# First block's attention by pairs of heads: two heads share TensorE's row halves and column halves, in steps of two units

## The chip, the core and the metric

One Trainium2 core runs the whole program in one launch. Its engines run on their own and meet through semaphores: TensorE (PE; PEld is its weight load), VectorE (DVE), ScalarE (ACT), GpSimd (POOL) and SyncE (SP), which issues the transfers. The metric is the device time of one execution in microseconds, the median of several.

## What is computed

Two transformer blocks, each two layers deep, on one sequence of 256 tokens of width 1024. The change touches the first block's attention alone. Cut to that:

```python
def attention(q, k, v, scale):          # 256 queries in blocks of 128
    def one_block(qi):
        s = jnp.einsum('bhgqd,bhkd->bhgqk', qi, k) * scale
        p = jax.nn.softmax(s, axis=-1)
        return jnp.einsum('bhgqk,bhkd->bhgqd', p, v)

for i in range(2):                       # first_block
    ...                                  # projections, norms, rope
    og = attention(qg, kg, vg, ...)      # GQA: 6 heads of 64, 2 key heads, 3 query heads to a key head
    om = attention(qm, km, vm, ...)      # MLA: 6 heads, 96 wide in q and k, 64 in v
    mix = concatenate([og, om, pooled]) @ w_out
```

In layer 0 attention is done twice: for the 256 context tokens (keys: the 256 context tokens) and for the 256 latent tokens (keys: all 512). In layer 1 only the latent tokens have queries. All of it is in float32.

## The kernel before

Every engine has its program written out in order; banks of PSUM (eight, 512 float32 wide) are handed out by `plan_banks` ahead of time, and an engine waits on a bank's semaphores `filled` and `drained`. Weights come through a ring of three 2 MB slots (`ring`), and SyncE issues the transfer into a slot when the last product of the slot's old weights has been issued.

Attention goes by **units**: one head, one set (context, or latent) and 128 queries. A set has 256 keys (two tiles of 128, context) or 512 (four tiles, latent). Layer 0 has 48 units (12 heads x 2 sets x 2 halves of the queries), layer 1 has 24. One unit passes through these stages, which the text names by letters:

- **S** (TensorE, L1229): scores, one product of 128 queries with 256 or 512 keys. A GQA head is 64 rows deep and lies in partitions 0 to 63 or 64 to 127 of `qT` and `kT` (`base = 64 * (h // 3)`); an MLA head is 96 rows deep.
- **R** (VectorE, L2024): the negative row maximum out of PSUM.
- **E** (ScalarE, L1599): exp with that maximum as bias, into `pb`, with the row sums; frees the score bank.
- **N** (VectorE, L2034, L2035): reciprocal of the sum, and scaling of the weights in `pb`.
- **T** (TensorE, L1241): the weights transposed, tile by tile.
- **C** (ScalarE, L1608): the transposed weights copied to `pT`.
- **V** (TensorE, L1255), once for two units (both halves of a head's queries): values, one product of 64 columns by 256 queries for each tile, accumulated.
- **O** (VectorE, L2044), once for two units: V's result copied to `mixT` (the same memory as `hT`).

The three loops run in steps of one unit. TensorE does S of unit u, T of unit u-2 and, every second step, V; VectorE R of u, N of u-1, O; ScalarE E of u, C of u-2. Scores have banks 0 to 2, transposes 3 and 4, values 5 and 6, by turns. In layer 0 TensorE also does eight rows of the modulation product in between (`mod_products`, L1066), each as two halves of four 512-column products, which write four strips of 32 columns; VectorE copies each row out (L1848). Bank 7 is theirs. A TensorE product in float32 shows as two matmul records (a transpose as one).

After attention follow, in layer 0, the transposed modulation rows (L1078), and in both layers the pooled part (L1268), the output projection (L1124) and the MLP.

Of the kernel before, what the change touches and what calls it, by code (L numbers as in the profile page):

```python
# [11 lines left out]
ALU = mybir.AluOpType  # L12
ACT = mybir.ActivationFunctionType
# [43 lines left out]
ATTN_STEPS = 6  # L57
# [120 lines left out]

def plan_banks():
# [24 lines left out]
    for i in range(DEPTH):  # L204
# [14 lines left out]
        u = 0  # L219
        pair = 0  # L220
        for h in range(GQ + MH):
            for s in range(len(sets_of(i))):
                for qt in range(2):
                    take((tag, "s", u), u % 3)
                    take((tag, "t", u), 3 + u % 2)
                    u += 1
                take((tag, "o", pair), 5 + pair % 2)
                pair += 1
# [154 lines left out]
def program(nc, A, out):  # L383
# [10 lines left out]
    with ExitStack() as ctx:  # L394
# [202 lines left out]
        def await_bank(eng, key):  # L597
            b, n = use[key]
            eng.wait_ge(filled[b], n + 1)

# [377 lines left out]
        def _(pe):  # L978
# [151 lines left out]
            for i in range(DEPTH):  # L1130
# [76 lines left out]
                sets = sets_of(i)  # L1207
                units = [(h, s, qt) for h in range(GQ + MH) for s in range(len(sets)) for qt in range(2)]
# [4 lines left out]
                ru[0] += len(units)  # L1213
                for s_ in range(len(units) + 4):
                    if s_ < len(units):
                        h, s, qt = units[s_]
                        if h == GQ and s == 0 and qt == 0:
# [4 lines left out]
                        q0, tiles = sets[s][0] + qt * P, sets[s][1]  # L1222
                        b = start_bank((tag, "s", s_))
                        if h < GQ:
                            base = 64 * (h // 3)
                            lhs, rhs = qT[base:base + HD, h % 3, q0:q0 + P], kT[base:base + HD, 0:tiles * P]
                        else:
                            lhs, rhs = qmT[0:MQK, h - GQ, q0:q0 + P], kmT[0:MQK, h - GQ, 0:tiles * P]
                        fill(mm(b[:, 0:tiles * P], lhs, rhs, start=True, stop=True), (tag, "s", s_))  # L1229


                    n, step = divmod(s_, ATTN_STEPS)
                    if i == 0 and n < MOD_ATTN and step in (2, 4):
                        mod_products(MOD_FIRST + n, range(0, 4) if step == 2 else range(4, KC))
                    u = s_ - 2
                    if 0 <= u < len(units):
                        h, s, qt = units[u]
                        b = start_bank((tag, "t", u))
                        pe.wait_ge(p_ready, p_base + u + 1)
                        for j in range(sets[s][1]):  # L1240
                            last = tr(b[:, j * P:(j + 1) * P], pb[:, u % 3, j * P:(j + 1) * P], IDENT)  # L1241
                        fill(last, (tag, "t", u))
                    u = s_ - 3
                    if 0 <= u < len(units) and u % 2 == 1:
                        h, s, _ = units[u]
                        pair = u // 2
                        b = start_bank((tag, "o", pair))
                        await_drained(pe, (tag, "t", u - 1))
                        await_drained(pe, (tag, "t", u))
                        base = 64 * (h % 2)  # L1250
                        tiles = sets[s][1]
                        for j in range(tiles):
                            v = v_tok[:, j, HD * (h // 3):HD * (h // 3) + HD] if h < GQ else \
                                vm_tok[:, j, MV * (h - GQ):MV * (h - GQ) + MV]
                            last = mm(b[base:base + 64, 0:SEQ], v, pT[:, pair % 2, j, :],  # L1255
                                      start=(j == 0), stop=(j == tiles - 1))
                        fill(last, (tag, "o", pair))
# [14 lines left out]
                npair = len(units) // 2  # L1272
                await_drained(pe, (tag, "o", npair - 1))
                await_drained(pe, (tag, "o", npair - 2))
# [173 lines left out]
        def _(act):  # L1448
# [116 lines left out]
            for i in range(DEPTH):  # L1565
# [20 lines left out]
                sets = sets_of(i)  # L1586
                units = [(h, s, qt) for h in range(GQ + MH) for s in range(len(sets)) for qt in range(2)]
                base = sum(24 * len(sets_of(j)) for j in range(i))
                for s_ in range(len(units) + 2):
                    if s_ < len(units):  # L1590
                        u = s_
                        h, s, qt = units[u]
                        keys = sets[s][1] * P
                        act.wait_ge(nmax_ready, base + u + 1)
                        if u >= 3:

                            await_bank(act, (tag, "t", u - 3))
                        st = stat[:, 8 * (u % 4):8 * (u % 4) + 8]
                        drain(act_fn(pb[:, u % 3, 0:keys], bank((tag, "s", u))[:, 0:keys], ACT.Exp, bias=st[:, 2:3],  # L1599
                                     accum_out=st[:, 4:5]), (tag, "s", u))  # L1600
                    u = s_ - 2
                    if 0 <= u:
                        h, s, qt = units[u]
                        tiles, pair = sets[s][1], u // 2
                        await_bank(act, (tag, "t", u))
                        if pair >= 2:
                            await_bank(act, (tag, "o", pair - 2))
                        drain(act_fn(pT[:, pair % 2, 0:tiles, qt * P:(qt + 1) * P],  # L1608
                                     bank((tag, "t", u))[:, 0:tiles * P].rearrange("p (j q) -> p j q", j=tiles),
                                     ACT.Copy), (tag, "t", u))  # L1610
# [162 lines left out]
        def _(dve):  # L1773
# [227 lines left out]
            for i in range(DEPTH):  # L2001
# [13 lines left out]
                sets = sets_of(i)  # L2015
                units = [(h, s, qt) for h in range(GQ + MH) for s in range(len(sets)) for qt in range(2)]
                for s_ in range(len(units) + 4):
                    if s_ < len(units):
                        u = s_
                        h, s, qt = units[u]  # L2020
                        keys = sets[s][1] * P
                        st = stat[:, 8 * (u % 4):8 * (u % 4) + 8]
                        await_bank(dve, (tag, "s", u))
                        V.tensor_reduce(st[:, 2:3], bank((tag, "s", u))[:, 0:keys], AX_X, ALU.max, negate=True)\  # L2024
                            .then_inc(nmax_ready, 1)
                    if i == 0 and s_ and s_ % ATTN_STEPS == 0 and s_ // ATTN_STEPS <= MOD_ATTN:
                        mod_row_copied(MOD_FIRST + s_ // ATTN_STEPS - 1)
# [232 lines left out]
```

## Time and profile before

| | |
|---|---|
| median of 3 runs | 2026.58 us (2022.17 to 2028.48) |
| profiled execution | 2027.55 us, its span 2025.7 us |
| busy in the span | PE 1897.6 us (94%), PEld 1499.4, DVE 1104.3, ACT 885.2, POOL 398.1 |
| attention of layer 0 | 193.2 to 306.9 us of the span |
| attention of layer 1 | 885.3 to 955.7 us of the span |

A matmul's record lasts until its last result is written, so records of one engine overlap: what an instruction costs TensorE is the distance to the next start. Granted clock 1.00 is 2.4 GHz, 0.50 is 1.2 GHz. A row's bracket says how long the engine was idle before it, and who released it.

### The profile page before, as it was taken

The page shows a single profiled execution, that of the slowest core. Times are in us where ns is not written, and L with a number is a line of the kernel's source. Part 1 is how long each engine was busy: PE and PEld are TensorE (multiplying, and loading weights), DVE is VectorE, ACT ScalarE, POOL GpSimd, SP SyncE. Part 2 cuts the span into 40 slices and gives each one's busy share as a digit, 9 for nine tenths or more (in the row PEclk, how much of TensorE's full clock was granted, in tenths as well). Part 3 has the DMA queues.
Part 4 walks back from the last instruction along what each step waited for, and adds up shares of the span by engine and source line. Part 5 has one row for each costly group of instructions (what it writes and reads, how often), then busy time and mean ns, then how long its engine had stood idle before and what let it go on. Part 6 is the DMA issues. An engine that isn't in the chain of part 4 may idle for free.

```text
span 2025.7 us, 28617 instructions
## 1 busy us (share of the span) xinstructions
PE 1897.6 (94%) x10840; PEld 1499.4 (74%) x10840; DVE 1104.3 (55%) x1948; ACT 885.2 (44%) x1757; POOL 398.1 (20%) x834
## 2 busy tenths in 40 slices
PE   4999999899999998999999989988999799989998
PEld 2443445388888885634899989877899798878898
DVE  3317551377777633354355557566555575665554
ACT  2226440242423333353355556455554364555542
POOL 1014100000000000140000006035453142254523
PEclk8899997899999999989899999999999899999999
DMA  8311440235455431300344532532244334323351
GB/s 297 127 51 42 158 165 2 83 136 197 168 191 182 166 83 32 117 1 1 116 176 172 197 131 95 207 126 84 97 154 169 123 137 166 126 84 126 126 171 59
DMA packets 139875, 255.26 MB, mean 126 GB/s; under 512 B 14926, under 2 KB 21724, under 8 KB 139612
## 3 DMA queue, kind: packets, MB, share of 16 engines
q1 hardware_dynamic: 138742, 251.16, 35.7%
q8 instruction: 88, 1.44, 0.3%
q0 software_dynamic: 704, 2.10, 0.3%
q14 instruction: 47, 0.39, 0.1%
q10 hardware_dynamic: 294, 0.18, 0.0%
HBM read 252.38 MB, written 1.05 MB: 125 GB/s over the span
## 4 chain that ended last, share of the span: by engine, by line
PE 82%; DVE 7%; ACT 4%; issue 3%; POOL 1%; SPq 1%; DMA 1%; ACTq 0%; DVEq 0%; POOLq 0%
PE ps L1115 16%; PE ps L1117 15%; PE ps L1116 15%; PE ps L1124 10%; PE ps L1009 3%; PE ps L1229 3%; PE ps L1255 3%; PE ps L1241 2%; PE ps L1026 1%; PE ps L1324 1%; PE ps L1326 1%; PE ps L1325 1%; PE ps L1089 1%; PE ps L1066 1%; SPq L790 1%
## 5 line engine op out<-in xcount | busy, mean ns | idle before, releaser
L1915 DVE TENSOR_TENSOR big_r<-ring,big_r 128x1024 fp32r<-128x1024 f32 x198 | 245.1, 1239 | 257.9 <-ACT big_r L1505 257.4
L1505 ACT ACTIVATE big_r<-ring 128x1024 fp32r<-128x1024 f32 x198 | 209.4, 1059 | 386.9 <-PE ps L1117 378.2
L1116 PE MATMUL ps<-big_r 128*128 128x256 f32 (+1 forms) x1120 | 374.0, 334 | 0.0
L1115 PE MATMUL ps<-hT_r,big_r 128*128 128x256 f32 (+1 forms) x896 | 290.8, 325 | 11.2 <-DVE big_r L1924 10.9
L1117 PE MATMUL ps<-hT_r,big_r 128*128 128x256 f32 (+1 forms) x896 | 283.4, 316 | 0.0
L1116 PEld LDWEIGHTS ps<-big_r 128*128 128x128 f32 x1120 | 215.2, 192 | 19.1
L1124 PE MATMUL ps<-hT,ring 128*128 128x512 f32 (+2 forms) x576 | 207.4, 520 | 10.7 <-ACT hT L1526 8.9
L1115 PE MATMUL ps<-big_r 128*128 128x256 f32 (+1 forms) x592 | 195.6, 330 | 1.4 <-DVE big_r L2070 1.4
L1117 PE MATMUL ps<-big_r 128*128 128x256 f32 (+1 forms) x592 | 194.6, 329 | 0.0
L1115 PEld LDWEIGHTS ps<-hT_r,big_r 128*128 128x128 f32 x896 | 173.1, 193 | 27.7 <-issue 11.8
L1124 PEld LDWEIGHTS ps<-hT,ring 128*128 128x128 f32 (+1 forms) x576 | 109.3, 192 | 105.7 <-issue 95.0
L1117 PEld LDWEIGHTS ps<-hT_r,big_r 128*128 128x128 f32 x896 | 173.2, 193 | 10.4
L1915 DVE TENSOR_TENSOR cst_r<-ring,w_ukv_sb_r 128x1024 fp32r<-128x1024 f32 x70 | 87.5, 1250 | 116.2 <-ACT w_ukv_sb_r L1505 116.2
L1115 PEld LDWEIGHTS ps<-big_r 128*128 128x128 f32 x592 | 112.5, 190 | 12.0 <-DVE big_r L2070 2.2
L1117 PEld LDWEIGHTS ps<-big_r 128*128 128x128 f32 x592 | 112.5, 190 | 10.0
L1881 DVE SCALAR_TENSOR_TENSOR pT<-ring,csilu,pT 128x512 f32<-128x512 f32 x168 | 118.5, 747 | 1.3
L1115 PE MATMUL ps<-hT_r,w_ukv_sb_r 128*128 128x256 f32 x384 | 114.6, 299 | 0.0
L894 POOL MEMSET big<- 128x1088 f32 x2 | 2.0, 1014 | 560.3 <-PE ps L1117 560.3
L1505 ACT ACTIVATE w_ukv_sb_r<-ring 128x1024 fp32r<-128x1024 f32 x70 | 74.1, 1058 | 85.4 <-PE ps L1117 72.6
L1117 PE MATMUL ps<-hT_r,cst_r 128*128 128x256 f32 x384 | 110.1, 287 | 0.0
L1116 PE MATMUL ps<-xT_r,w_ukv_sb_r 128*128 128x256 f32 x384 | 110.0, 286 | 0.0
L1898 DVE SCALAR_TENSOR_TENSOR nt<-ps,nt 128x256 f32<-128x256 f32 (+3 forms) x74 | 39.0, 527 | 125.3 <-ACT nt L1477 125.0
(278 smaller groups left out, 4205.7 us busy)
## 6 DMA issues: line engine op xcount, KB each, us to landing
ring<-in_w_in SPq DMA_DIRECT2D x42, 2048.0 KB, 7.8
ring<-in_w_mlp SPq DMA_DIRECT2D x32, 2048.0 KB, 7.8
ring<-in_w_mod SPq DMA_DIRECT2D x24, 2048.0 KB, 8.0
ring<-in_w_out SPq DMA_DIRECT2D x4, 2048.0 KB, 8.1
ring<-in_w_out_a SPq DMA_DIRECT2D x4, 2048.0 KB, 7.8
ring<-in_w_out_b SPq DMA_DIRECT2D x4, 2048.0 KB, 7.9
ring<-in_w_o SPq DMA_DIRECT2D x4, 2048.0 KB, 8.4
ring<-in_w_in SPq DMA_DIRECT2D x12, 256.0 KB, 5.0
```

Of the source, the lines that this page charges most:

```text
L1009: last = mm(b[0:parts, 0:T], ones, sq[0:parts, n % SQ, 0:T], start=(j == 0), stop=(j == chunks - 1))
L1115: mm(b[:, 0:T], w_hi[:, k, :], hi(k), start=(k == 0), stop=False)
L1116: mm(b[:, 0:T], w_hi[:, k, :], lo(k), start=False, stop=False)
L1117: last = mm(b[:, 0:T], w_lo[:, k, :], hi(k), start=False, stop=(k == KC - 1))
L1124: last = mm(b[0:cols, 0:T], w[:, k, m:m + cols], src(k), start=(k == 0), stop=(k == KC - 1))
L1229: fill(mm(b[:, 0:tiles * P], lhs, rhs, start=True, stop=True), (tag, "s", s_))
L1241: last = tr(b[:, j * P:(j + 1) * P], pb[:, u % 3, j * P:(j + 1) * P], IDENT)
L1255: last = mm(b[base:base + 64, 0:SEQ], v, pT[:, pair % 2, j, :], start=(j == 0), stop=(j == tiles - 1))
L1505: act_fn(hi, raw, ACT.Copy).then_inc(hi_ready, 1)
L1881: ins = V.scalar_tensor_tensor(acc, w, c, acc, ALU.mult, ALU.add)
L1898: drain(V.scalar_tensor_tensor(r2, bank(key)[0:parts, 0:T], width * EPS, r2, ALU.add, ALU.mult), key)
L1915: V.tensor_tensor(lo, raw, hi.bitcast(F32), ALU.subtract).then_inc(lo_ready, 1)
```

## The change

Attention now goes by **groups** (two heads, one set) in **steps** (one half of the group's queries, so two units, one of each head). The GQA pairs are heads h and h+3, whose rows are the two halves of the partitions and which belong to different key heads; the MLA pairs are neighbours. A step's two S are issued back to back into two banks. V takes both heads of a group, tile by tile in turn, into the two halves of one bank's partitions (an even head 0 to 63, an odd one 64 to 127). Scores have banks 0 to 3, transposes 4 and 5, values bank 6 alone. The fourth buffer for weights is a part of `sq`; the transposed weights of odd groups go to `rstd` and `nt`, which ScalarE may overwrite once the last MLA key unit is drained, for which it now waits at the start. O of a GQA group is two copies of 64 partitions, of an MLA group one of 128. ScalarE does C of step j-2 ahead of E of step j; before, E came first. The modulation halves come at the second and third of every three steps.

```diff
-ATTN_STEPS = 6
+ATTN_STEPS = 3
...
+HEAD_PAIRS = [(h, h + GQ // 2) for h in range(GQ // 2)] + [(GQ + h, GQ + h + 1) for h in range(0, MH, 2)]
+def groups_of(i):
+    return [(pair, s) for pair in HEAD_PAIRS for s in range(len(sets_of(i)))]
...
+        for u in range(4 * len(groups_of(i))):
+            take((tag, "s", u), u % 4)
+            take((tag, "t", u), 4 + u % 2)
+        for g in range(len(groups_of(i))):
+            take((tag, "o", g), 6)
...
+        def weights(u):
+            return pb[:, u % 4, :] if u % 4 < 3 else sq[:, 2, :]
+        def weights_T(g, e):
+            return pT[:, e, :, :] if g % 2 == 0 else (rstd, nt)[e][:, :, :].rearrange("p a (b c) -> p (a b) c", b=2)
...
+                for j in range(steps + 3):
+                    if j < steps:
+                        pair, s = groups[j // 2]
...
+                        q0, tiles = sets[s][0] + j % 2 * P, sets[s][1]
+                        banks = [start_bank((tag, "s", 2 * j + e)) for e in range(2)]
+                        for e, h in enumerate(pair):
+                            if h < GQ:
+                                rows = slice(HD * (h // 3), HD * (h // 3) + HD)
+                                lhs, rhs = qT[rows, h % 3, q0:q0 + P], kT[rows, 0:tiles * P]
...
+                            fill(mm(banks[e][:, 0:tiles * P], lhs, rhs, start=True, stop=True), (tag, "s", 2 * j + e))
...
+                    n, step = divmod(j, ATTN_STEPS)
+                    if i == 0 and n < MOD_ATTN and step:
+                        mod_products(MOD_FIRST + n, range(0, 4) if step == 1 else range(4, KC))
+                    if 0 <= j - 2 < steps:
+                        tiles = sets[groups[(j - 2) // 2][1]][1]
+                        for u in (2 * j - 4, 2 * j - 3):
+                            b = start_bank((tag, "t", u))
+                            pe.wait_ge(p_ready, p_base + u + 1)
...
+                    g, odd = divmod(j - 4, 2)
+                    if 0 <= g < len(groups) and not odd:
...
+                        for t in range(tiles):
+                            for e, h in enumerate(pair):
+                                rows = slice(64 * (h % 2), 64 * (h % 2) + 64)
...
+                                last = mm(b[rows, 0:SEQ], v, weights_T(g, e)[:, t, :], start=(t == 0), stop=(t == tiles - 1))
...
+                await_drained(act, (tag, f"km{MH - 1}", 0))
+                for j in range(steps + 2):
+                    if j >= 2:
...
+                        for e in range(2):
+                            key = (tag, "t", 2 * j - 4 + e)
+                            await_bank(act, key)
...
+                    if j < steps:
...
+                            act.wait_ge(nmax_ready, base + u + 1)
...
+                for j in range(steps + 3):
+                    if j < steps:
+                        keys = sets[groups[j // 2][1]][1] * P
+                        for u in (2 * j, 2 * j + 1):
...
+                            await_bank(dve, (tag, "s", u))
...
+                    if 1 <= j <= steps:
...
+                        for u in (2 * j - 2, 2 * j - 1):
...
+                            await_drained(dve, (tag, "s", u))
...
+                    g, odd = divmod(j - 4, 2)
+                    if 0 <= g < len(groups) and not odd:
...
+                        await_bank(dve, key)
+                        if pair[0] < GQ:
+                            for h in pair:
+                                rows = slice(64 * (h % 2), 64 * (h % 2) + 64)
+                                last = V.tensor_copy(mixT[rows, h // 2, q0:q0 + SEQ], bank(key)[rows, 0:SEQ])
+                        else:
+                            last = V.tensor_copy(mixT[:, pair[0] // 2, q0:q0 + SEQ], bank(key)[:, 0:SEQ])
```

TensorE's order in the GQA heads of layer 1, before (a pair of units; `x4` are four transposes or the four tiles of V):

```order
L1229 MATMUL ps<-big 128x512
L1241 MATMUL ps<-cst,pb 128x128 x4
L1229 MATMUL ps<-big 128x512
L1241 MATMUL ps<-cst,pb 128x128 x4
L1255 MATMUL ps<-pT,big 64x256 x4
```

and of the change, one group, at the same place (S is L1243, T is L1255, V is L1269; this group's transposed weights are those of `pT`):

```order
L1243 MATMUL ps<-big 128x512 x2
L1255 MATMUL ps<-cst,pb 128x128 x4
L1255 MATMUL ps<-cst,sq 128x128 x4
L1243 MATMUL ps<-big 128x512 x2
L1255 MATMUL ps<-cst,pb 128x128 x8
L1269 MATMUL ps<-pT,big 64x256 x8
```

Two S stand together, two units' transposes stand together, and V's eight products of a group stand where four of a head stood.

VectorE's order at the same place, before (two heads):

```order
L2024 TENSOR_REDUCE stat<-ps 128x1
L2034 RECIPROCAL stat<-stat 128x1
L2035 TENSOR_SCALAR pb<-pb,stat 128x512
L2044 COPY hT<-ps 64x256
L2024 TENSOR_REDUCE stat<-ps 128x1
L2034 RECIPROCAL stat<-stat 128x1
L2035 TENSOR_SCALAR pb<-pb,stat 128x512
```

and of the change (R is L2034, N is L2043 and L2044, O is L2055):

```order
L2034 TENSOR_REDUCE stat<-ps 128x1 x2
L2043 RECIPROCAL stat<-stat 128x1
L2044 TENSOR_SCALAR pb<-pb,stat 128x512
L2043 RECIPROCAL stat<-stat 128x1
L2044 TENSOR_SCALAR sq<-sq,stat 128x512
L2055 COPY hT<-ps 64x256 x2
L2034 TENSOR_REDUCE stat<-ps 128x1 x2
L2043 RECIPROCAL stat<-stat 128x1
L2044 TENSOR_SCALAR pb<-pb,stat 128x512
L2043 RECIPROCAL stat<-stat 128x1
L2044 TENSOR_SCALAR pb<-pb,stat 128x512
```

R of a step's two units now stands ahead of both N of the step before, and O's two copies follow every second N pair.

## Rows read from the trace of the kernel before

**Rows 1.** Windows: stretch, busy us by engine (instructions), granted clock, DMA share, GB/s.

```profile
193.20:307.00 113.80, 109.48 (x514) 50.27 (x514) 65.57 (x177) 51.04 (x145) 17.95 (x23) 1.00 0.42 148
...
885.30:898.00 12.70, 12.61 (x23) 4.97 (x22) 6.17 (x14) 4.28 (x11) 9.74 (x15) 0.50 0.00 0
898.00:955.70 57.70, 54.49 (x220) 27.42 (x219) 28.63 (x71) 26.29 (x62) 0.00 (x0) 0.98 0.00 1
```

**Rows 2.** TensorE's timeline, layer 1, GQA: start, us, engine, line, shapes, [idle].

```profile
906.12 1.12 PE L1229 MATMUL ps<-big 64*128 64x512 f32 x2
907.18 0.66 PE L1241 MATMUL ps<-cst,pb 128*128 128x128 f32 x4
907.76 1.12 PE L1229 MATMUL ps<-big 64*128 64x512 f32 x2
...
909.42 1.92 PE L1255 MATMUL ps<-pT,big 128*64 128x256 f32 x8
911.28 1.12 PE L1229 MATMUL ps<-big 64*128 64x512 f32 x2
```

**Rows 3.** The same, layer 1, MLA; the last row two pairs later.

```profile
921.56 1.12 PE L1229 MATMUL ps<-big 96*128 96x512 f32 x2
922.52 0.60 PE L1241 MATMUL ps<-cst,pb 128*128 128x128 f32 x4
922.96 1.02 PE L1229 MATMUL ps<-big 96*128 96x512 f32 x2
...
931.84 1.12 PE L1229 MATMUL ps<-big 96*128 96x512 f32 x2
```

**Rows 4.** TensorE's timeline, layer 0, GQA, around a half modulation row (L1066).

```profile
226.54 0.44 PE L1241 MATMUL ps<-cst,pb 128*128 128x128 f32 x2
226.90 0.70 PE L1229 MATMUL ps<-big 64*128 64x256 f32 x2
227.53 1.07 PE L1066 MATMUL ps<-ring,cwide 128*32 128x512 f32 x8
228.53 0.66 PE L1241 MATMUL ps<-cst,pb 128*128 128x128 f32 x4
229.11 1.08 PE L1255 MATMUL ps<-pT,big 128*64 128x256 f32 x4
230.12 0.70 PE L1229 MATMUL ps<-big 64*128 64x256 f32 x2
```

**Rows 5.** The same, layer 0: latent V of one head and of the ninth after.

```profile
213.95 1.94 PE L1255 MATMUL ps<-pT,big 128*64 128x256 f32 x8
...
297.56 1.94 PE L1255 MATMUL ps<-pT,big 128*64 128x256 f32 x8
```

**Rows 6.** TensorE's timeline, second block: two 64-row products, what comes next.

```profile
1314.06 0.37 PE L1399 MATMUL ps<-big 64*128 64x128 f32 x1
1314.07 0.37 PE L1400 MATMUL ps<-big 64*128 64x128 f32 x1
...
1314.48 0.23 PE L1401 MATMUL ps<-mask_bf,ident_bf 128*128 128x128 bf16 x1
```

**Rows 7.** VectorE's timeline, layer 1, MLA: R, reciprocal, scaling, O.

```profile
933.00 0.69 DVE L2024 TENSOR_REDUCE stat<-ps 128x1 f32<-128x512 f32 x1 [2.08 <-PE ps L1229]
933.61 0.15 DVE L2034 RECIPROCAL stat<-stat 128x1 f32<-128x1 f32 x1
933.80 0.49 DVE L2035 TENSOR_SCALAR pb<-pb,stat 128x512 f32<-128x512 f32 x1
934.20 0.41 DVE L2044 COPY hT<-ps 64x256 f32<-64x256 f32 x1
```

**Rows 8.** ScalarE's timeline at the same place: E, C.

```profile
933.73 0.69 ACT L1599 ACTIVATE pb<-ps,stat 128x512 f32<-128x512 f32 x1 [2.10 <-DVE stat L2024]
...
934.41 0.59 ACT L1608 ACTIVATE pT<-ps 128x512 f32<-128x512 f32 x1
```

More of the change, by code:

```diff
@@ L1204, in _ @@
                 run_units(tag, units_a(i) + units_m(i), main)
-                sets = sets_of(i)
-                units = [(h, s, qt) for h in range(GQ + MH) for s in range(len(sets)) for qt in range(2)]
+                sets, groups = sets_of(i), groups_of(i)
+                steps = 2 * len(groups)
                 pe.wait_ge(roped, roped_before(tag, 1))
@@ L1212, in _ @@
                 p_base = ru[0]
[L1213 to L1217, printed above, removed]
+                ru[0] += 2 * steps
+                for j in range(steps + 3):
+                    if j < steps:
+                        pair, s = groups[j // 2]
+                        if pair[0] == GQ and s == 0 and j % 2 == 0:
                             pe.wait_ge(roped, roped_before(tag, 1) + 2 * MH)
@@ L1229, in _ @@
[L1229 to L1250, printed above, removed]
-                        tiles = sets[s][1]
[L1252 to L1257, printed above, removed]
+                        q0, tiles = sets[s][0] + j % 2 * P, sets[s][1]
@@ new lines, in _ @@
+                    n, step = divmod(j, ATTN_STEPS)
[7 more added lines that the diff above has]
+                            for t in range(tiles):
+                                last = tr(b[:, t * P:(t + 1) * P], weights(u)[:, t * P:(t + 1) * P], IDENT)
+                            fill(last, (tag, "t", u))
@@ L1270, in _ @@
                     fill(last, key)
[L1272 to L1274 removed]
+                await_drained(pe, (tag, "o", len(groups) - 1))
                 await_drained(pe, (tag, "pool", 1))
@@ L1584, in _ @@
                 run_units(tag, units_a(i) + units_m(i))
-                sets = sets_of(i)
-                units = [(h, s, qt) for h in range(GQ + MH) for s in range(len(sets)) for qt in range(2)]
+                sets, groups = sets_of(i), groups_of(i)
+                steps = 2 * len(groups)
                 base = sum(24 * len(sets_of(j)) for j in range(i))
[L1589 to L1610, printed above, removed]
@@ L2014, in _ @@
                 run_units(tag, units_a(i) + units_m(i))
[L2015 to L2027, printed above, removed]
-                    u = s_ - 1
-                    if 0 <= u < len(units):
-                        h, s, qt = units[u]
-                        keys = sets[s][1] * P
-                        st = stat[:, 8 * (u % 4):8 * (u % 4) + 8]
-                        await_drained(dve, (tag, "s", u))
-                        link(V.reciprocal(st[:, 6:7], st[:, 4:5]))
-                        V.tensor_scalar(pb[:, u % 3, 0:keys], pb[:, u % 3, 0:keys], st[:, 6:7], None, ALU.mult)\
-                            .then_inc(p_ready, 1)
-                    u = s_ - 4
-                    if 0 <= u and u % 2 == 1:
-                        h, s, _ = units[u]
@@ L2046, in _ @@
+                        drain(last, key)
                 if i == 0:
```

58 lines of the change are left out of this document (37 added, 21 removed).

## Prediction

> **What bounds the kernel now.** I read the windows first, then TensorE's timeline in steady attention, then VectorE's and ScalarE's. The letters S, R, E, N, T, C, V, O are those of the section on the kernel. In layer 0's attention (113.8 us) TensorE is busy 109.48 us, VectorE 65.57 and ScalarE 51.04; in layer 1's (12.7 + 57.7 us) TensorE is busy 67.1 us, VectorE 34.8, ScalarE 30.6 [rows 1]. What has to be seen next is whether that busy time is work. It is: in a GQA pair of layer 1 every phase starts where the one before has issued its columns, S 1.06 us, T 0.58, S, T, then V 1.86, a pair of units in 5.16 us [rows 2]. MLA has the same period, (931.84 - 921.56) / 2 = 5.14 us, with S 0.96 and T 0.44 [rows 3]. Layer 0 shows the short pieces: T of two tiles 0.36, S of 256 columns 0.63, half a modulation row 1.00, V of two tiles 1.01 [rows 4], and a whole head, its share of the eight modulation rows included, takes (297.56 - 213.95) / 9 = 9.29 us [rows 5]. Twelve heads are 111.5 us of the 113.7 from 193.2 to 306.9; twelve pairs are 61.8 us of layer 1's 70.4. So attention is bound by what TensorE issues, the rest being ends and, in layer 1, a start at half clock. What shortens S and V shortens the kernel; what shortens VectorE or ScalarE does not.
>
> **The GQA scores.** Heads h and h+3 stand in the two row halves, and their two S are now issued back to back into two banks. The trace has that form elsewhere: the second block's two 64-row score products start 0.01 us apart, and the next instruction starts 0.42 us after the first [rows 6]; one after the other, two products of 128 columns would have taken that twice less one change of phase. I therefore take a GQA pair's S at the price of one: 1.06 us (latent set) or 0.63 (context set). The other bound is two in a row, which is rival A. MLA's S fills 96 rows and stays double: at most 2 x 0.96 = 1.92, and for 256 columns 0.10 less than the GQA form, 2 x 0.53 = 1.06.
>
> **The values.** Two heads go to column halves, interleaved tile by tile. No row shows two 64-column products side by side, but the half modulation row is four 512-column products into four strips of 32 columns in 1.00 us [rows 4], where one 512-column S alone takes 1.06 [rows 2]. So column strips share the time of one. Bounds: 1.86 for both heads (one price) and 3.72 (no sharing); I take 1.86, the strip row being nearly the same operation, and 1.01 for the context set.
>
> **The transposes.** Their number is unchanged, but two units now stand together. The second costs what tiles alone add: 0.58 - 0.36 = 0.22 for two tiles [rows 2, 4], 0.44 for four, against 0.36 and 0.58 apart. A step's T is 1.02 (latent) or 0.58 (context); in MLA I take 0.88 for one step and 1.02 for the one that goes before V.
>
> **The sum for TensorE.** A group is two heads of one set: two steps of S, two of T, one V.
> GQA, latent: 2 x 1.06 + 2 x 1.02 + 1.86 = 6.02 us (before: 10.32).
> GQA, context: 2 x 0.63 + 2 x 0.58 + 1.01 = 3.43.
> MLA, latent: 2 x 1.92 + 0.88 + 1.02 + 1.86 = 7.60 (before: 10.28).
> MLA, context: 2 x 1.06 + 2 x 0.58 + 1.01 = 4.29.
> Layer 0: 3 x (6.02 + 3.43) + 3 x (7.60 + 4.29) + 16 half rows x 1.00 = 80.0 us against 111.5: -31.5.
> Layer 1: 3 x 6.02 + 3 x 7.60 = 40.9 against 61.8: -20.9.
>
> **What the other queues then do.** VectorE's work hardly changes. From R to the reciprocal is 0.61 us, on to the scaling 0.19, on to the next 0.40, and a copy is 0.41 [rows 7]: a GQA latent group is 4 x 1.20 + 2 x 0.41 = 5.62 us, under 6.02. ScalarE's is 4 x (0.68 + 0.59) = 5.08 [rows 8]. In layer 0 their 65.57 and 51.04 us stand against 80. Both fit, but with little to spare in the three GQA groups of layer 1.
>
> What is queued behind each wait matters more. VectorE does R of step j+1 before N of step j, and every second step waits with O for V. Take a V that ends at time 0, with S of step j+1 behind it. R can begin 1.16 us after that S is issued (933.00 - 931.84 [rows 3, 7]); the two O copies, 0.82 us, lie inside these 1.16. R, R, reciprocal, scaling: 1.16 + 1.22 + 0.19 + 0.49 = 3.06 us until the first weights of step j are ready, 3.65 for the second. TensorE wants them after S, T, S: 1.06 + 1.02 + 1.06 = 3.14, and the second 0.44 later, at 3.58. So the transposes come within a tenth of a microsecond of waiting; with semaphore time I charge 0.3 us to each of the six GQA latent groups, 1.8 in all. In MLA TensorE arrives at 1.92 + 0.88 + 1.92 = 4.72 and waits for nothing; in layer 0 a half row lies in two steps of three and covers it, except beside a step without one. The other step parity has V in between. Four score banks let S of step j+2 wait only for E of step j, which ends more than a step earlier; the two transpose banks are drained by C within the next S and T. The single value bank is emptied two steps before its next use.
>
> ScalarE's new wait for the last MLA key unit costs nothing: VectorE drains that unit ahead of its first R in its own queue. The modulation slots are consumed every 10 us instead of 14, three deep, and the queue's 148 GB/s of that window [rows 1] becomes some 200. The last released slots belong to the output projection and are asked for several steps before the end.
>
> The start of layer 1 does change. Before, the clock is 0.50 (1.2 GHz) while only S and T run, and 0.98 on average from 898.0 on, where the first V begins [rows 1]. In the new order five steps' S and three steps' T lie ahead of the first V: 5 x 1.06 + 3 x 1.02 = 8.4 us, at half clock 16.7, against 12.7 before. If V is what raises the clock, that is about 4 us more at half rate, 2 us lost; if paired S raises it too, nothing. I take 1.0.
>
> Sum: -31.5 - 20.9 + 1.8 + 1.0 = -49.6. The profiled execution took 2027.55 us (span 2025.7), so 1978.0; the median of the runs is 1.0 lower, so **1977 us**.
>
> **Rivals.** *A, row halves take turns.* Then each GQA step pays S twice: 12 latent steps x 0.96 and 6 context steps x 0.53 give 14.7 us back: 1992. [Rows 6] speak against it. If the column halves took turns, 12 latent groups x 1.86 and 6 context groups x 1.01 give 28.4 back: 2005, and the strips in [rows 4] speak against that. Chance of either 0.05.
>
> *B, VectorE's queue sets the pace.* Margins of a tenth cannot be trusted: if each link of R, E, N and T is 0.2 us longer than in the rows, or VectorE runs slower beside GpSimd, TensorE waits about 0.8 us in each of the 18 groups: 14 us, 1991; spread 1987 to 2002. For it: 5.62 against 6.02. Against it: in MLA and in layer 0, where most of the gain is, TensorE still has 1 to 2 us of slack in a group. The Trainium skill, TensorEngine Tiling (Array Packing), section PSUM Bottleneck, warns of this very turn: packing speeds TensorE up and not the emptying of PSUM. [...] Chance 0.22.
>
> *C, slower: the clock falls inside attention.* The work is thinner in products and thicker in transposes: T takes 34% of a GQA group (2.04 of 6.02) where it took 22% (1.16 of 5.16). If TensorE then stayed at 1.2 GHz through both stages, the 80.0 and 40.9 us would double: 160 against 113.7 and 82 against 70.4, 58 us more than before: 2085. It decides from where some 50 of the 121 us run at half clock, since each costs another. For it: 885.3 to 898.0, when TensorE was busy 12.61 of 12.70 us with S and T at 0.50 [rows 1]. Against it: layer 0 holds 1.00 throughout with the same S, T and V, and each S and V now fills the whole array. The Trainium skill, TensorE: Matmul & The Clock Gate, Part 4 on transposes, says that a transpose does not count as busy for the clock as a product does; the trace's stretch before 898 fits that. Chance 0.04.
>
> *D, better than the sum.* The rows' prices contain a change of phase (S 1.06 against 0.96 in MLA), and a second S behind a first need not pay it. With 0.1 us less for each of some 60 phases, no stall and no late clock: 1969, at best 1964. Chance 0.08.
>
> **How the numbers follow.** The forecast's own case, 1967 to 1987, has 0.61. The range 1965 to 1992 adds most of D, A and half of B: about 0.8. Faster by over 0.3% (6 us, about what a measurement of this kernel can tell from no change) are all cases but C and a worse B: 0.94; within 0.3%: 0.02; slower: 0.04.
>
> **What would show it.** In the new trace the two GQA S must start together and be followed by T some 1.06 us later; V of two heads must take some 1.9 us for 16 matmul records of the latent set; a GQA latent group must last 6.0 to 6.4 us, an MLA one 7.4 to 7.7; layer 0's attention some 84 us, layer 1's some 50. Waits of T for the scaling above 0.5 us in every group would be B, a granted clock under 1.00 after layer 1's first 17 us C. I am wrong if time saved here returns later, which I see no wait for: the stages behind find their weights in the ring.

## The result, and the profile after

The changed kernel takes 1971.37 us (median of 4 runs, 1969.74 to 1972.63), the kernel before in the same session 2027.53 us (2022.17 to 2029.32): a ratio of 0.9727, 95% interval 0.9707 to 0.9747, 56.2 us less. Forecast were 1977 us and 49.6 us less, range 1965 to 1992. The profiled execution after has a span of 1967.9 us.

Where the time went, from the starts in the two timelines (attention counts from its first S to what follows it: the turned modulation rows in layer 0, the pooled part in layer 1), in us:

| stage | before | after | difference |
|---|---|---|---|
| run's start to the first block's first projection | 62.49 | 58.83 | -3.7 |
| from there to attention, layer 0 | 130.77 | 131.58 | +0.8 |
| attention, layer 0 | 113.60 | 83.51 | -30.1 |
| turned modulation rows | 11.64 | 12.05 | +0.4 |
| pooled part and output projection, layer 0 | 77.36 | 76.89 | -0.5 |
| MLP of layer 0, projections of layer 1 | 489.46 | 490.25 | +0.8 |
| attention, layer 1 | 70.33 | 45.72 | -24.6 |
| the rest | 1070.06 | 1069.08 | -1.0 |

The two attentions are 54.7 us less, and nothing comes back later. The first row lies ahead of anything that was edited, and its 3.7 us are chance: in the kernels further down, which begin with the same instructions, that stretch takes between 59.2 and 63.1 us.

The windows of the changed kernel, beside [rows 1] (columns as there; the first row is all of layer 0's attention, the second the turned modulation rows, the other three layer 1's attention):

```profile
190.40:273.90 83.50, 79.70 (x512) 39.28 (x512) 64.75 (x170) 48.07 (x144) 17.38 (x22) 1.00 0.57 202
273.90:285.60 11.70, 11.67 (x66) 11.55 (x64) 0.42 (x1) 0.00 (x0) 0.00 (x0) 0.60 0.01 4
853.10:857.60 4.50, 3.72 (x9) 1.21 (x9) 2.45 (x5) 1.47 (x5) 4.06 (x8) 0.61 0.00 0
857.60:865.50 7.90, 6.87 (x36) 3.42 (x36) 7.69 (x19) 6.69 (x17) 5.69 (x8) 1.00 0.00 1
865.50:898.80 33.30, 31.82 (x197) 19.02 (x196) 23.32 (x59) 21.10 (x52) 0.00 (x0) 1.00 0.00 1
```

The instruction counts are those of before (512 against 514 matmul records in layer 0), but TensorE is busy 79.70 us instead of 109.48: the same products, side by side. VectorE and ScalarE do nearly the same work (64.75 and 48.07 us, before 65.57 and 51.04) in 30 us less, and TensorE is still the engine that is busy nearly all the time. The third row holds the one term whose sign the forecast had wrong: at the start of layer 1 the clock is 0.61 on average for 4.5 us, where it was 0.50 for 12.7.

The profile models the ends of TensorE's records, so the prices below are distances from start to start. TensorE's timeline in the same place shows the new order (start, us, then the instruction; layer 1, the GQA groups and the first MLA step):

```profile
853.12 3.71 PE L1243 MATMUL ps<-big 64*128 64x512 f32 x8
857.61 1.13 PE L1243 MATMUL ps<-big 64*128 64x512 f32 x4 [0.79 <-ACT pb L1620]
859.26 1.40 PE L1255 MATMUL ps<-cst,pb 128*128 128x128 f32 x8 [0.52 <-DVE pb L2044]
860.59 1.13 PE L1243 MATMUL ps<-big 64*128 64x512 f32 x4
...
863.15 1.13 PE L1243 MATMUL ps<-big 64*128 64x512 f32 x4
864.39 1.22 PE L1255 MATMUL ps<-cst,pb 128*128 128x128 f32 x8
865.53 1.95 PE L1269 MATMUL ps<-pT,big 128*64 128x256 f32 x16
867.41 1.13 PE L1243 MATMUL ps<-big 64*128 64x512 f32 x4
868.47 0.65 PE L1255 MATMUL ps<-cst,pb 128*128 128x128 f32 x4
868.96 0.60 PE L1255 MATMUL ps<-cst,sq 128*128 128x128 f32 x4
869.40 1.88 PE L1243 MATMUL ps<-big 96*128 96x512 f32 x4
```

Four records of S, two heads, take 868.47 - 867.41 = 1.06 us, what two records took in [rows 2]. Sixteen records of V, two heads, take 867.41 - 865.53 = 1.88 us, what eight took. From S at 863.15 to S at 869.40 lie two S, two T of four tiles for each head, and one V, the work of a whole latent GQA group: 6.25 us, where 6.02 and, with waits, 6.0 to 6.4 were forecast. An MLA group further on:

```profile
873.97 1.98 PE L1243 MATMUL ps<-big 96*128 96x512 f32 x4
875.79 0.60 PE L1255 MATMUL ps<-cst,pb 128*128 128x128 f32 x4
876.23 0.60 PE L1255 MATMUL ps<-cst,sq 128*128 128x128 f32 x4
876.66 1.88 PE L1243 MATMUL ps<-big 96*128 96x512 f32 x4
878.38 1.04 PE L1255 MATMUL ps<-cst,pb 128*128 128x128 f32 x8
879.35 1.95 PE L1269 MATMUL ps<-pT,big 128*64 128x256 f32 x16
```

S 1.82 and 1.72, T 0.87 and 0.97, V 1.88 (to the next S at 881.23): 7.26 us, where two periods of [rows 3] took 10.28.

### The profile page after: what moved, and what is told of

It reads as the page before. It is cut to its first block, busy times and chain, and to the rows that moved or that the text cites. A ratio compares the mean times of both kernels' runs of the same rounds, so it can differ in the third digit from the quotient of the medians.

```text
span 1967.9 us, 28606 instructions
## 1 busy us (share of the span) xinstructions
PE 1840.9 (94%) x10840; PEld 1477.3 (75%) x10840; DVE 1101.7 (56%) x1939; ACT 881.7 (45%) x1757; POOL 397.6 (20%) x834
## 4 chain that ended last, share of the span: by engine, by line
PE 80%; DVE 8%; ACT 5%; issue 3%; POOL 1%; SPq 1%; DMA 1%; ACTq 0%; DVEq 0%; POOLq 0%
PE ps L1128 16%; PE ps L1130 15%; PE ps L1129 15%; PE ps L1137 10%; PE ps L1022 3%; PE ps L1243 2%; PE ps L1269 1%; PE ps L1039 1%; PE ps L1255 1%; PE ps L1335 1%; PE ps L1336 1%; PE ps L1337 1%; PE ps L1102 1%; SPq L803 1%; DVE big_r L1926 1%
## 5 line engine op out<-in xcount | busy, mean ns | idle before, releaser
L1128 PE MATMUL ps<-hT_r,big_r 128*128 128x256 f32 (+1 forms) x896 | 290.9, 325 | 10.9 <-DVE big_r L1935 10.6
L1137 PE MATMUL ps<-hT,ring 128*128 128x512 f32 (+2 forms) x576 | 207.2, 519 | 10.8 <-ACT hT L1537 9.2
```

The source lines that it names most:

```text
L1128: mm(b[:, 0:T], w_hi[:, k, :], hi(k), start=(k == 0), stop=False)
L1137: last = mm(b[0:cols, 0:T], w[:, k, m:m + cols], src(k), start=(k == 0), stop=(k == KC - 1))
```

## The experiments

"Attention stages" below are the two rows of the table, together 129.2 us in the changed kernel; medians are beside the changed kernel's 1971.37, ratios against the kernel before on the same chip.

### Which half is worth what

**One column half.** Both heads' values go into one half of the partitions, one head after the other:

```diff
-                        for t in range(tiles):
-                            for e, h in enumerate(pair):
-                                rows = slice(64 * (h % 2), 64 * (h % 2) + 64)
+                        for e, h in enumerate(pair):
+                            for t in range(tiles):
+                                cols = slice(SEQ * e, SEQ * e + SEQ)
...
-                                last = mm(b[rows, 0:SEQ], v, weights_T(g, e)[:, t, :], start=(t == 0), stop=(t == tiles - 1))
+                                last = mm(b[0:64, cols], v, weights_T(g, e)[:, t, :], start=(t == 0), stop=(t == tiles - 1))
...
```

> V of a group's two heads goes to the same column half (partitions 0 to 63, one head in columns 0 to 255 of the bank, the other behind it); everything else is as in the change. Theory (TensorE's columns are the bound and the halves share their time): V costs twice, 12 latent groups x 1.72 us and 6 context groups x 0.86, about +26 us against the change, near 1997. Rival (the order in steps of two and the fewer phases bring the gain, not the sharing): within 5 us of the change.

Measured: 1994.26 us (1993.69 to 1999.84), ratio 0.9859 [0.9815, 0.9903]; attention 99.74 and 56.01 us, 26.5 more. Its TensorE timeline, an MLA group of layer 1:

```profile
891.94 1.94 PE L1269 MATMUL ps<-rstd,big 128*64 128x256 f32 x8
893.71 1.89 PE L1269 MATMUL ps<-nt,big 128*64 128x256 f32 x8
895.53 1.98 PE L1243 MATMUL ps<-big 96*128 96x512 f32 x4
897.36 0.60 PE L1255 MATMUL ps<-cst,pb 128*128 128x128 f32 x4
897.79 0.60 PE L1255 MATMUL ps<-cst,sq 128*128 128x128 f32 x4
898.23 1.88 PE L1243 MATMUL ps<-big 96*128 96x512 f32 x4
899.95 1.04 PE L1255 MATMUL ps<-cst,pb 128*128 128x128 f32 x8
900.92 1.29 PE L1269 MATMUL ps<-pT,big 128*64 128x256 f32 x5
```

V now takes 3.59 us (891.94 to 895.53) against 1.88. Twelve latent groups of 1.71 are 20.5 us. A context V takes 1.87 us (221.23 to 223.10) against 1.01, and six of them are 5.2. Layer 0 also has 3.4 us at half clock (202.9 to 206.3) that the changed kernel does not have, at most 1.7 us. The column halves share fully, as [rows 4] said.

**Row pairs undone.** The GQA pairs are neighbours, so both heads lie in the same row half in two groups of three (the pair 2, 3 lies in both halves; it stands second here):

```diff
-HEAD_PAIRS = [(h, h + GQ // 2) for h in range(GQ // 2)] + [(GQ + h, GQ + h + 1) for h in range(0, MH, 2)]
+HEAD_PAIRS = [(0, 1), (2, 3), (4, 5)] + [(GQ + h, GQ + h + 1) for h in range(0, MH, 2)]
```

> GQA pairs are heads (0,1), (2,3), (4,5): only (2,3) spans both row halves, the other two pairs' S take turns. Theory: 8 latent steps x 0.85 and 4 context steps x 0.43 give 8.5 us back; and, because layer 1 now opens with S of one row half, its clock stays at 0.50 well beyond the 3 us that it takes in the change, some 4 to 6 us more: +13 in all, near 1984. Rival on the clock (it rises after a fixed time whatever S does): +8.5 and the clock up after about 3 us as in the change. Rival on S (row halves bring nothing): no change.

Measured: 1983.19 us (1979.84 to 1984.98), ratio 0.9803 [0.9766, 0.9841]; attention 94.95 and 51.52 us, 17.2 more.

**The same, with the shared pair first**, so that attention starts with S in both row halves:

```diff
-HEAD_PAIRS = [(h, h + GQ // 2) for h in range(GQ // 2)] + [(GQ + h, GQ + h + 1) for h in range(0, MH, 2)]
+HEAD_PAIRS = [(2, 3), (0, 1), (4, 5)] + [(GQ + h, GQ + h + 1) for h in range(0, MH, 2)]
```

> The same three pairs with (2,3) first, so that layer 1 opens with paired S. Both clock theories: +8.5 us against the change and the clock up about 3 us after attention's start in layer 1. The difference to the run with (0,1) first is what paired S at the start is worth to the clock: 4 to 6 us by the theory, 0 by the rival.

Measured: 1976.6 us (1974.67 to 1978.82), ratio 0.9773 [0.9735, 0.9811]; attention 88.19 and 47.49 us, 6.5 more. S of a pair that lies in one row half, from its timeline in layer 1:

```profile
866.62 1.98 PE L1243 MATMUL ps<-big 64*128 64x512 f32 x4
868.53 0.66 PE L1255 MATMUL ps<-cst,pb 128*128 128x128 f32 x4
```

That is 1.91 us where two S side by side take 1.06, the 0.85 a latent step that was expected. Eight latent and four context steps would be 8.5 us; where the missing 2 us went was not traced. Two of rival A's three pairs would be 9.8 us; 6.5 puts all three at some 10.

The two kernels do the same products in another order, and differ by 10.8 us. Windows of the first of them at the start of layer 1, where its first S starts at 863.53:

```profile
865.00:870.00 5.00, 5.00 (x8) 2.35 (x8) 2.07 (x3) 1.77 (x5) 4.56 (x8) 0.50 0.00 0
870.00:875.00 5.00, 4.84 (x15) 2.35 (x14) 4.13 (x10) 2.36 (x6) 3.48 (x5) 0.50 0.00 0
875.00:880.00 5.00, 5.00 (x17) 2.12 (x14) 3.68 (x11) 3.88 (x11) 0.00 (x0) 0.75 0.00 2
```

and of the second, where it starts at 859.15:

```profile
857.60:863.00 5.40, 5.21 (x12) 1.68 (x10) 1.86 (x4) 1.44 (x4) 4.96 (x9) 0.54 0.00 0
863.00:870.00 7.00, 6.36 (x25) 3.32 (x26) 6.82 (x16) 5.16 (x14) 6.24 (x9) 1.00 0.00 1
```

TensorE is busy without a gap in the first row of the first, and stays at 1.2 GHz; with two S side by side it is back at 2.4 GHz some 4 us after attention began. In layer 0, which the expectation left out, the first kernel also falls to half clock just behind its first S, for some 20 us (0.50 from 191.5 to 212.0, with TensorE busy throughout), and the second keeps 1.00. The clock is the difference that the two profiles show; whether the other order of the pairs costs anything besides is not shown. One more profile of each, unchanged:

> A second profile of the kernel that opens each layer with S of one row half. Theory (paired S raises the clock, S of one half does not): layer 1 again at 0.50 for 10 us or more after attention's start. Rival (the stretch at half clock is an accident of the moment): a stretch of another length, as short as 3 us.

> A second profile of the kernel that opens each layer with paired S. Theory: in layer 1 the clock is up within some 5 us of attention's start, and layer 0 stays at 1.00. Rival: any length up to 15 us.

Measured, one run each: 1983.8 and 1981.6 us; attention 94.95 and 49.87 us, against 89.09 and 47.49: 5.9 and 2.4 us apart, the same sign in both layers, smaller. In layer 1 the clock was low for some 10 and 7 us around the first S, and back 8.0 and 3.7 us behind it: the second is what the theory expected, the first falls short of its 10 us. In layer 0 the first kernel has its 20 us again; the second has 3.4 us at half clock (202.9 to 206.3), where the theory had 1.00 throughout. The medians of several runs above differ by 6.6 us.

All thirteen profiles of this case bear on the start of layer 1. Where it opens with two S side by side and the clock is low at the first S (eight profiles), the clock is back 1.8 to 4.2 us behind it; where it opens with S of one row half (the kernel before and both profiles of the first kernel here), 15.0, 14.0 and 8.0 us behind it. Two more open with paired S at full clock, and it falls later. Nor does S of one row half always bring the clock down: in layer 0 of the kernel before, where single S stand between modulation rows, T and V, it stays at 1.00.

**Both undone:**

> Both sharings mostly undone at once, the schedule kept: V of both heads in one column half, and GQA pairs (2,3), (0,1), (4,5), of which only the first spans both row halves. If the costs simply add: what the run with one column half gave back and what the run with (2,3) first gave back, +26 + 6 = some +32 us against the change, near 2002, which leaves some 20 to 25 us below the kernel before that neither sharing explains (joined phases, fewer waits, the start of layer 1). Rival (the halves are all of it): +50 us or more, at the kernel before within 0.5%.

Measured: 2003.87 us (2001.33 to 2005.38), ratio 0.988 [0.9845, 0.9916]; attention 103.58 and 57.78 us, 32.1 more than in the changed kernel. The parts nearly add up: 26.5 and 6.5. And this kernel, in which no two products of a pair of heads run together except in one GQA pair of three, is still 22.6 us under before in attention (161.4 against 183.9). One part of that is read from the MLA group above: 895.53 - 891.94 for V, 1.83 and 1.72 for S, 0.87 and 0.97 for T are 8.98 us, where [rows 3] have 10.28. S and T of two units stand together, and a phase that is twice as long is changed half as often: 1.3 us in each MLA latent group. The other part is layer 1's clock, low for 6.8 us around the first S instead of 17.0; within attention that is 3.7 us at half rate instead of 15.0, some 5.6 us less lost.

### Order and depth

**V head by head**, still in both column halves:

```diff
-                        for t in range(tiles):
-                            for e, h in enumerate(pair):
+                        for e, h in enumerate(pair):
+                            for t in range(tiles):
```

> V's two heads still go to the two column halves, but all tiles of the first head are issued before the second head's. Theory (products start in program order, so only the neighbours at the seam share): nearly as in the run with one column half, +20 to +26 us. Rival (TensorE runs the other half's products ahead): within 3 us of the change.

Measured: 1980.17 us (1977.28 to 1983.38), ratio 0.9791 [0.9753, 0.9829]; attention 89.01 and 51.17 us, 11.0 more. Neither theory gave that number. Its timeline, one V of layer 1 (`rstd` holds the first head's weights, `nt` the second's):

```profile
877.97 1.29 PE L1269 MATMUL ps<-rstd,big 128*64 128x256 f32 x5
878.89 0.43 PE L1269 MATMUL ps<-nt,big 128*64 128x256 f32 x1
879.10 0.38 PE L1269 MATMUL ps<-rstd,big 128*64 128x256 f32 x1
879.16 0.38 PE L1269 MATMUL ps<-nt,big 128*64 128x256 f32 x1
...
879.59 1.24 PE L1269 MATMUL ps<-nt,big 128*64 128x256 f32 x5
880.76 1.98 PE L1243 MATMUL ps<-big 96*128 96x512 f32 x4
```

Each head has eight records, one every 0.22 us. The second head's first starts with the first head's fifth, 0.92 us after V began, four records ahead of its turn; from there both run side by side, and the second head's last ones run alone. V takes 2.79 us: 0.91 more than tile by tile, and 12 x 0.91 = 10.9. In the context set, four records a head, V takes 1.02 us against 1.01, which fits a reach of four records. So what shares is decided by the order of issue within a few records, not by the halves alone.

**One step in flight.** TensorE does T of step j-1 and ScalarE C of j-1, and V and O come one step earlier:

```diff
-                    if 0 <= j - 2 < steps:
-                        tiles = sets[groups[(j - 2) // 2][1]][1]
-                        for u in (2 * j - 4, 2 * j - 3):
+                    if 0 <= j - 1 < steps:
+                        tiles = sets[groups[(j - 1) // 2][1]][1]
+                        for u in (2 * j - 2, 2 * j - 1):
...
-                    g, odd = divmod(j - 4, 2)
+                    g, odd = divmod(j - 3, 2)
...
```

> One step in flight instead of two: T of step j-1 and V of the group that ended at step j-2 follow S of step j; C and O move up by one step as well. Theory (the chain T, C, E, N, T is some 3.4 us long and a GQA latent step of TensorE 3.0, and N of a step stands behind R of the next): TensorE waits 0.4 to 1 us in most latent steps and at every start, +6 to +14 us against the change. Rival (TensorE alone sets the pace, the second step in flight is idle): within 3 us.

Measured: 2035.02 us (2030.98 to 2037.55, 7 runs), ratio 1.0056 [1.0031, 1.0080]: slower than the kernel before, and far outside what I expected. Attention 122.99 and 68.96 us, 62.7 more. The wait is in its timeline, an MLA group of layer 1:

```profile
938.33 0.63 PE L1255 MATMUL ps<-cst,pb 128*128 128x128 f32 x4 [1.47 <-DVE pb L2044]
...
939.39 1.88 PE L1243 MATMUL ps<-big 96*128 96x512 f32 x4
942.74 1.22 PE L1255 MATMUL ps<-cst,pb 128*128 128x128 f32 x8 [1.47 <-DVE pb L2044]
```

and in the list of what T waited for (idle us, times; in the changed kernel 2.5 us, 5 times):

```profile
  DVE pb L2044: 48.1, 35
```

Scaling of step j-1 stands on VectorE behind R of step j, and R of step j waits for S of step j. T of j-1, which is next on TensorE after that same S, therefore waits for S, R, R, reciprocal and scaling in a row, in 35 of the 36 steps. I had counted only the work of the second step and not the order of VectorE's queue. The waits are 48.1 of the 62.7 us. Beside them the clock falls: its mean is 0.90 from 193 to 318 us and 0.93 from 904 to 976, where the changed kernel has 1.00 nearly throughout; how much of the other 14.6 us that makes is not shown.

### Whether VectorE sets the pace

**A row maximum more in every step** (it goes to a spare column, and nothing reads it):

```diff
+                            if u % 2 == 0:
+                                V.tensor_reduce(st[:, 3:4], bank((tag, "s", u))[:, 0:keys], AX_X, ALU.max)
```

> VectorE does one more row maximum in each step (into a spare column): 12 context steps x 0.34 and 24 latent steps x 0.61 us, 18.7 us of added VectorE work in attention. Theory (TensorE is the bound, VectorE close only in the GQA groups of layer 1 and in the two starts): +3 to +7 us against the change, MLA groups as long as before. Rival (VectorE's queue sets the pace): +15 to +19 us.

Measured: 1974.57 us (1971.71 to 1980.07), ratio 0.9773 [0.9736, 0.9811]; attention 88.06 and 47.15 us, 6.0 more for 36 reductions, 24 of which cost VectorE 0.60 us and 12 some 0.35. Over half of the 6.0 is a stretch in layer 0 at a clock of 0.59, in its windows:

```profile
190.40:199.00 8.60, 6.47 (x38) 2.04 (x36) 8.46 (x20) 4.93 (x16) 8.21 (x12) 0.98 0.43 137
199.00:207.00 8.00, 6.97 (x38) 3.00 (x36) 6.43 (x17) 3.55 (x10) 7.53 (x9) 0.59 0.32 118
```

0.41 of 8.0 us are 3.3; 2.7 us are left for 18.6 us of added work. Whether the added work brought that stretch about is not shown: two profiles without it have 3.4 us at half clock in the same place. In MLA the group stays at 7.26 us, from S to S in TensorE's timeline:

```profile
882.64 1.98 PE L1243 MATMUL ps<-big 96*128 96x512 f32 x4
...
889.90 1.98 PE L1243 MATMUL ps<-big 96*128 96x512 f32 x4
```

VectorE does not set the pace of the MLA groups, and over all groups the added work costs a small part of its length. The Trainium skill, TensorEngine Tiling (Array Packing), section PSUM Bottleneck, says that packing does not speed up the emptying of PSUM, and that this may become the bottleneck after a fourfold speedup of TensorE. Here two products of S or V run side by side and not four, and it did not become the bound: VectorE is busy 64.75 of 83.50 us after the change.

**GpSimd's pooled sums later.** They wait until half of attention's row maxima are done, so that the first groups have VectorE undisturbed:

```diff
                 nc.gpsimd.memset(upad[:, :, :, :], 0.0).then_inc(padded, 1)
...
+                pool.wait_ge(nmax_ready, sum(24 * len(sets_of(j)) for j in range(i)) + 12 * len(sets_of(i)))
```

> GpSimd's pooled sums wait until half of the row maxima are done, so that VectorE starts attention without GpSimd beside it; the sums are still ready before they are needed. Theory (attention's first 12 us in layer 0, where VectorE is busy 11.8 of 12.3 us and a scaling of 256 columns takes up to 1.67 us, are held up by GpSimd's work beside VectorE): -1.5 to -4 us against the change, all of it in the first two groups of each layer. Rival (the start is a chain of latencies and GpSimd only coincides): 0.

Measured: 1968.06 us (1966.33 to 1969.99, 6 runs), ratio 0.9733 [0.9707, 0.9758]; attention 82.05 and 44.44 us, 2.7 less. VectorE's first scaling in layer 0, from the timeline of the changed kernel:

```profile
192.64 1.67 DVE L2044 TENSOR_SCALAR pb<-pb,stat 128x256 f32<-128x256 f32 x1
```

and of this one:

```profile
195.18 0.62 DVE L2045 TENSOR_SCALAR pb<-pb,stat 128x256 f32<-128x256 f32 x1
```

The profile shows the gain in attention, and the interval of the ratio overlaps the changed kernel's. Layer 0 holds 1.5 us of the 2.7, where the scaling is faster. In layer 1, the other 1.3, the clock was also back 1.8 us behind the first S instead of 3.5, so that part is not VectorE's alone.

### A version that beats both

**Modulation rows turned inside attention.** After attention of layer 0 the changed kernel has 12 us in which TensorE only turns modulation rows, the clock falls to 0.60, and the pooled part and the projection begin below full clock. Here, with the last edit, each of the eight modulation rows is turned in four products of two columns (eight records; the expectation's 64 are records too) ahead of a V, into idle columns of its bank:

```diff
+TURN_AT = (1, 2, 4, 5, 7, 8, 10, 11)
...
+            def mod_turned(n):
...
+                for m in range(4):
+                    at = SEQ + 2 * (4 * n + m)
+                    last = mm(ps[:, 6, at:at + 2], mod_row(MOD_FIRST + n)[:, m * P:(m + 1) * P], four[:, :], start=True,
+                              stop=True)
...
+                        if i == 0 and g in TURN_AT:
+                            n = TURN_AT.index(g)
...
+                            last = mod_turned(n)
...
-                    mod_transposed(MOD_FIRST, MOD_FIRST + MOD_ATTN, "modB")
...
```

> The change with GpSimd's pooled sums later, and with the eight modulation rows of layer 0 transposed inside attention, each just before a V in the idle columns of V's bank, instead of 64 two-column products in a row behind attention. Theory (those 11.7 us at a granted clock of 0.60 become some 7 us of attention at 1.00, and without them the clock does not fall before the output projection, whose first stretch ran at 0.50): attention of layer 0 +6 to +8 us, the stage behind it -11, the projection -8 to -14: -12 to -18 us against the change. Rival (the clock falls anyway in the waits at attention's end): -4 to -6 us.

Measured: 1960.79 us (1958.45 to 1964.72, 5 runs), ratio 0.967 [0.9644, 0.9697]: faster than both, by 10.6 us against the changed kernel, a little under what I expected. Attention of layer 0 takes 89.38 us (5.9 more), the turning 12.05 less, pooled part and projection 72.55 (4.3 less), layer 1's attention 0.7 less. The windows behind the turned rows in the changed kernel:

```profile
285.60:290.00 4.40, 3.11 (x7) 2.06 (x8) 1.15 (x3) 0.00 (x0) 0.00 (x0) 0.50 0.00 0
290.00:300.00 10.00, 9.11 (x16) 3.79 (x15) 0.75 (x1) 0.00 (x0) 0.00 (x0) 0.66 0.00 0
```

and behind attention here:

```profile
281.00:296.00 15.00, 13.19 (x33) 5.93 (x33) 2.38 (x4) 0.63 (x1) 0.00 (x0) 1.00 0.00 0
296.00:320.00 24.00, 24.00 (x57) 10.64 (x56) 3.50 (x8) 3.15 (x4) 0.00 (x0) 1.00 0.27 88
```

The clock stays at 1.00 through the projection's beginning. Against the kernel with the last edit alone, attention of layer 0 is 7.3 us longer by the rows turned inside it, and the turning took 11.5 us there, so moving them is worth 11.5 - 7.3 = 4.2 us. Pooled part and projection are 4.9 us shorter than there (4.3 than in the changed kernel), less than the 8 to 14 expected; that this is the clock is read from the rows above and not shown apart.

## Why the prediction was right

The forecast's own case came: 49.6 us less, 56.2 measured.

*Row halves.* S of a pair at the price of one, 1.06: measured 1.06. A second pair of S does take turns when both lie in one row half: 1.91 us for one such pair, and undoing two pairs of three cost 6.5 us, all three some 10, where rival A's half had 14.7. [Rows 6], one instance in another block with 128 columns, were enough.

*Column halves.* V of two heads at 1.86: measured 1.88. Undone, +26.5 against rival A's 28.4. The strips of [rows 4] were the right neighbour. What they could not tell is that the order tile by tile, which the modulation product has too, is part of the price: head by head half of the overlap is lost in the latent set.

*Transposes and MLA groups.* 7.60 forecast, 7.26 measured: S 1.82 and 1.72 for 1.92 each, T 0.97 ahead of V for 1.02. A second S behind a first pays no change of phase; rival D had the sign, 0.3 us a group.

*Layer 0.* 80.0 + some 4 us of ends and waits forecast as "some 84", 83.51 measured; -30.6 (with its share of the charged waits) against -30.1. The groups of the GQA heads are slower at the start, beside GpSimd, and those of MLA are faster.

*Waits of T.* I charged 1.8 us; T's waits for the scaling are 2.5 us in five places, all in both layers together (5.1 in ten places before). With 0.2 for the weights in `sq` rival B was worth 2.7 us, at the two starts and once at the end of layer 1, and not the 14 of every group.

*The step that was off: the start of layer 1.* I put five steps' S and three steps' T ahead of the first V at half clock and took +1.0, the middle of "V raises the clock" and "paired S raises it too". The first does not hold: the clock is at 1.00 from 857.6 on, 4.5 us behind the first S and 8 us ahead of the first V, before any T. The stretch lost 4.5 x (1 - 0.61) = 1.8 us, the one of before 12.7 x 0.5 = 6.4: -4.6 instead of +1.0, which is 5.6 us. Before, the clock stayed at 0.50 until 900.3, 2.3 us into the next row, and with that the term is -5.7. Layer 1 was 24.6 us less instead of 20.9 - 0.9 - 1.0 = 19.0. That this is 5.6 too is luck: MLA's three groups gave 1.0 more than forecast, and some 2 us came back in waits and ends that are not split here. The sign of the term was wrong, since I bounded it from below by nothing: a gain against before, in which S of one row half kept the clock down, was left out. The kernels with other GQA pairs bear out that S side by side is what ends the stretch: the same products, S of one row half first, and the clock of layer 1 stays low for 14 us from the first S in one profile, for 8 us in a second.

*Rival C* did not come: T takes 34% of a group, and the clock holds 1.00 in layer 0 throughout and in layer 1 from 857.6 on. It is not proof against every fall: of the other profiles with paired S first and two steps in flight, two show 3.4 us and one 6.8 us at half clock in layer 0. Nor do the two arguments beside it stand as written: MLA's S does not fill the array but 96 rows of it, and the stretch before 898 opens with six records of S alone, from 885.34 to 890.91, at half clock before any transpose.

Settled by runs are the two halves, the order, the depth, VectorE's part in MLA, and that the clock at the start of layer 1 comes back sooner with paired S first. Argued from one timeline only is how the 22.6 us that are left with neither half divide between joined phases and the clock. Open is why two profiles of one kernel have low stretches of 17 and of 10 us around the same S.

## What to carry to other kernels

A bound found as "TensorE is busy all the time" can still give way where its products use half the rows or columns: a row of the same operation elsewhere in the trace prices the pair, and the partners must stand next to each other in the order of issue. Then look at the depth: with work joined into larger steps a chain through another engine's queue needs two steps in flight, or the whole gain is lost in one wait per step. And price a clock's fall in both directions: an edit that fills the array sooner may end a slow stretch that the kernel before had.

## What the runs showed of the hardware

- Score products of one row half left TensorE at 1.2 GHz in layer 1 for 15.0, 14.0 and 8.0 us from the first S in three profiles, though it was busy nearly without a gap (the row 865.00:870.00 above is one of them); two side by side, begun at 1.2 GHz, had it at 2.4 GHz 1.8 to 4.2 us after the first in eight.
- A product for the other column half started four records ahead of its turn, and in these runs no more: 2.79 us for V head by head, 1.88 tile by tile, 3.59 without halves.
- A scaling of 256 columns on VectorE took 1.67 us beside GpSimd's sums, 0.62 at the same place with the sums later, and 0.35 at its least.
